# Attention probabilities transposed by a matmul with a diagonal matrix of row factors, in place of scaling on GpSimd and a transpose

## The reference

```
s = jnp.einsum('bhqd,bkhd->bhqk', qb, k) * scale      # plus bias / mask
p = softmax(where(valid, s, NEG))                     # exp(s - max) / sum
o = jnp.einsum('bhqk,bkhd->bqhd', p, v)               # o = g * (p @ v) in sel and win
```

## Time and profile before

| | us |
|---|---|
| median of 3 runs | 1456.19 |
| lowest and highest of them | 1454.94, 1457.26 |
| the profiled execution | 1460.9 |
| its span, first to last instruction | 1459.1 |
| attention of layer 0, first scores to last value product | about 101 to 160 |
| attention of layer 1, the same | about 830 to 875 |

### The profile page before, as it was taken

The page is one execution under the profiler, slowest core; times in us unless marked ns, Lnnn a source line. Parts: engine busy times, 40 slices in busy tenths (PEclk is TensorE's granted clock), DMA queues, the critical chain, the costliest instruction groups (busy, mean ns, idle before and its releaser), DMA issues.

```text
span 1459.1 us, 21577 instructions
## 1 busy us (share of the span) xinstructions
PE 1392.6 (95%) x8612; PEld 863.6 (59%) x8612; DVE 505.1 (35%) x834; ACT 356.4 (24%) x878; POOL 119.1 (8%) x155
## 2 busy tenths in 40 slices
PE   8977999999999999989999999999999999999878
PEld 3465576565656566654488466665656565666543
DVE  0387352333323323222610236232323323232253
ACT  1137132222222222212110242222222222222121
POOL 1229220000000000000100152100000000000000
PEclk9978999999999999999999989999999999999999
DMA  9540338999999999998563504599999999999951
GB/s 311 170 171 1 117 144 355 422 420 421 421 420 422 420 421 420 421 420 337 172 227 123 226 1 173 189 422 420 421 420 421 420 421 421 421 421 420 421 208 58
DMA packets 80806, 461.87 MB, mean 317 GB/s; under 512 B 9168, under 2 KB 9392, under 8 KB 30544
## 3 DMA queue, kind: packets, MB, share of 16 engines
q1 hardware_dynamic: 78128, 452.07, 76.3%
q0 software_dynamic: 2592, 8.53, 1.9%
HBM read 459.52 MB, written 1.05 MB: 316 GB/s over the span
## 4 chain that ended last, share of the span: by engine, by line
PE 90%; DVE 4%; POOL 2%; ACT 1%; issue 1%; DMA 0%; SPq 0%; DVEq 0%; ACTq 0%
PE ps L937 31%; PE ps L965 16%; PE ps L979 9%; PE ps L907 8%; PE ps L1083 4%; PE ps L644 4%; PE ps L688 3%; PE ps L803 3%; POOL roped L508 2%; PE ps L820 2%; PE ps L848 2%; PE ps L673 1%; PE ps L788 1%; PE ps L857 1%; PE ps L947 1%
## 5 line engine op out<-in xcount | busy, mean ns | idle before, releaser
L937 PE MATMUL ps<-ring,proj 128*64 128x256 f32 x2048 | 228.4, 381 | 5.9 <-issue 5.9
L965 PE MATMUL ps<-ring,qkT 128*64 128x512 f32 x1024 | 233.8, 598 | 0.0
L937 PEld LDWEIGHTS ps<-ring,proj 128*64 128x64 f32 x2048 | 152.2, 138 | 91.0 <-issue 25.4
L1693 DVE TENSOR_TENSOR o_tok<-ps,o_tok 128x1024 f32<-128x1024 f32 x128 | 156.6, 1224 | 103.8 <-PE ps L979 103.5
L1699 DVE TENSOR_TENSOR y_lo<-ps,y_hi 128x1024 fp32r<-128x1024 f32 x64 | 78.4, 1225 | 234.4 <-ACT y_hi L1283 234.4
L1685 DVE SCALAR_TENSOR_TENSOR roped<-roped,rows,ps 128x256 f32<-128x256 f32 x64 | 30.7, 480 | 318.1 <-ACT roped L1256 318.1
L965 PEld LDWEIGHTS ps<-ring,qkT 128*64 128x64 f32 x1024 | 67.8, 136 | 111.8 <-issue 110.4
L979 PE MATMUL ps<-y_hi,selT 128*128 128x512 f32 x256 | 113.2, 442 | 11.0 <-DVE o_tok L1693 7.5
L937 PE MATMUL ps<-ring,pT 128*64 128x256 f32 x1024 | 121.5, 379 | 2.2 <-ACT gb_row L1250 2.2
L1283 ACT ACTIVATE y_hi<-ps 128x1024 fp32r<-128x1024 f32 x64 | 65.5, 1024 | 234.5 <-PE ps L965 234.5
L937 PE MATMUL ps<-ring,gb_row 128*64 128x256 f32 x1024 | 121.5, 379 | 0.0
(11 more groups left out here) (247 smaller groups left out, 1497.2 us busy)
## 6 DMA issues: line engine op xcount, KB each, us to landing
ring<-in_exp_w_dram SPq DMA_DIRECT2D x384, 1024.0 KB, 13.4
ring<-in_od_w_in_dram SPq DMA_DIRECT2D x6, 2048.0 KB, 8.3
ring<-in_ple_w_gate_dram SPq DMA_DIRECT2D x4, 2048.0 KB, 11.1
ring<-in_ev_w_in_dram SPq DMA_DIRECT2D x3, 2048.0 KB, 21.5
ring<-in_sh_w_dram SPq DMA_DIRECT2D x6, 1024.0 KB, 7.0
ring<-in_ev_w_o_dram SPq DMA_DIRECT2D x2, 2048.0 KB, 10.7
ring<-in_od_w_o_dram SPq DMA_DIRECT2D x2, 2048.0 KB, 8.4
ring<-in_ev_w_in_dram SPq DMA_DIRECT2D x2, 1024.0 KB, 9.8
```

The lines of the kernel that those rows point to most:

```text
L937: ins = pe.matmul(ps[b * SLOTS:(b + 1) * SLOTS, 2, w * FE:(w + 1) * FE], xe(odd, c)[:, u * P + b * SLOTS:u * P + (b + 1) * SLOTS], views[b ...
L965: ins = pe.matmul(ps[b * SLOTS:(b + 1) * SLOTS, 4 + half, :], hT[:, f, b * SLOTS:(b + 1) * SLOTS], views[b][:, f, half * PIECE:(half + 1) ...
L1693: dve.tensor_tensor(y_acc[:, t, :], ps[:, bank:bank + 2, :].rearrange("p b n -> p (b n)"), y_acc[:, t, :], ALU.add)\
```

## The change

GpSimd no longer touches the scores. It builds, for each unit, four 128x128 diagonal matrices with the row factors on the diagonal, in one instruction: the identity, repeated four times, times `coef`, spread along the rows. Two such sets of four exist (`diag`, in `o_tok`, which is free in attention), so from the third unit on GpSimd also waits until TensorE has used the set of the unit before last. TensorE multiplies the block of unscaled probabilities (stationary) by the diagonal (moving), which gives the transposed and scaled block in the place where the transpose put it. The number of blocks, their PSUM places and the order of steps stay. DVE's guard on `coef` waits for the diagonal in place of the scaling.

```
-                for v, (what, t, g) in enumerate(UNITS[L % 2]):
-                    K = n_keys(t)
+                for v in range(len(UNITS[L % 2])):
                     pool.wait_ge(sem("sc_coef"), FIRST_UNIT[L] + v + 1)
-                    for s in range(4):
-                        part = scores[:, v % 4, s * K:(s + 1) * K]
-                        ins = pool.tensor_scalar(part, part, coef[:, v % 4, s:s + 1], None, ALU.mult)
-                    ins.then_inc(sem("sc_scaled"), 1)
+                    if v >= 2:
+
+                        pool.wait_ge(sem("unit_tp"), FIRST_UNIT[L] + v - 1)
+                    pool.tensor_tensor(diag[:, v % 2, :, :], ident.unsqueeze(1).to_broadcast([P, 4, P]),
+                                       coef[:, v % 4, :].unsqueeze(2).to_broadcast([P, 4, P]), ALU.mult)\
+                        .then_inc(sem("diag_built"), 1)
...
-                        pe.wait_ge(sem("sc_scaled"), B + v + 1)
+                        pe.wait_ge(sem("diag_built"), B + v + 1)
...
-                                ins = pe.transpose(ps[:, 4 + b // 4, (b % 4) * P:(b % 4 + 1) * P],
-                                                   scores[:, v % 4, s * n_keys(t) + c * P:s * n_keys(t) + (c + 1) * P],
-                                                   ident)
+                                ins = pe.matmul(ps[:, 4 + b // 4, (b % 4) * P:(b % 4 + 1) * P],
+                                                scores[:, v % 4, s * n_keys(t) + c * P:s * n_keys(t) + (c + 1) * P],
+                                                diag[:, v % 2, s, :], start=True, stop=True)
...
-                            dve.wait_ge(sem("sc_scaled"), B + v - 3)
+                            dve.wait_ge(sem("diag_built"), B + v - 3)
```

More of the change, by code:

```diff
@@ L173, in build_trunk @@
         y_acc = o_tok
+        diag = o_tok[:, 0, :].rearrange("p (u s n) -> p u s n", u=2, s=4)
         tmp_o = sb("tmp_o", 512)[:, :]
```

## The result

| | before | after |
|---|---|---|
| median, us | 1458.21 (15 runs) | 1461.62 (15 runs) |
| lowest and highest | 1454.94, 1462.52 | 1459.6, 1465.49 |
| the profiled execution | 1460.9 | 1460.05 |
| its span | 1459.1 | 1458.2 |
| layer 0, first scores to first product of the shared expert | 76.96 | 80.32 |

A forecast was written before the change was run, and what follows sets the result against it. TensorE was taken to make 90% of the chain, with GpSimd's scalings bounding part of layer 0's attention. Layer 0 +2.2 and layer 1 -1.4 gave +0.8 on 1456.19: 1457.0 us, range 1454.0 to 1460.7.

The forecast's parts named there:

- Start of layer 0, -1.1: Layer 0's first diagonal, taken at 1.27 us, is ready sooner than the scaled scores, so TensorE's first product starts 1.1 us earlier.
- Rival 2: Building the diagonal on GpSimd takes 2.87 us; layer 0 +2.9, layer 1 +2.0, total +4.9, 1461.1 us; chance 6%.
- The price of a product: On TensorE, products replacing transposes add 0.4 us per tile 0 unit, 0.87 per tile 1 unit, 0.7 at low clock.
- Idle time taken up, -4.7: In layer 0 the added TensorE work fills 4.7 of 5.9 us of its idle time, leaving 1.2.
- The tail, +1.75: From layer 0's output projection on, TensorE has no idle time, so units 10 and 11 add 1.75 us.
- Layer 0 together: Sum of layer 0's attention steps: +2.3 us, or +2.1 following each unit through all engines; taken as +2.2.
- Layer 1: Layer 1's attention: -2.4 us if the clock never falls, taken as -1.4 because timed runs may differ in clock falls.
- What lies outside, 0: After attention the chain is TensorE's to the end, so a shift passes through one to one, adding nothing.
- The base: The kernel before was taken at 1456.19 us, the median of three runs spread over 2.3 us.
- Rival 1: The clock brings no gain in layer 1; total +2.9 us, or +4.4 if earlier timed runs mostly had no fall; 14%.
- Rival 3: A product costs only a transpose's time on TensorE; layer 0 -2.6, layer 1 -7, 1446.6 us; chance 4%.
- Rival 4: Products keep the clock up where transposes do not; layer 0 +1.3, total about -1.1, 1455.1 us; chance 6%.

The follow-up runs named there:

- layer 0's half: The change in the 12 units of layer 0 alone, layer 1 as in the kernel before; ratios to before 1.0005, 1.0006 and 1.0004.
- products without diagonals: Kernel before, GpSimd still scaling, with only the transposes turned into products with the identity; ratio 1.0044, +6.4 us.
- filled kernel: Kernel before plus three unread 128x512 products in TensorE's idle time ahead of layer 1's first transpose; ratio 0.998 (-2.9 us), again 0.9984 (-2.3 us).

## Why the prediction was wrong

By its own steps:

- **Start of layer 0, -1.1.** The diagonal was taken at 1.27 and takes 1.04; the first product starts 9.31 us after the first scores, not 10.69. It was -1.4; 0.2 of the 0.3 beyond the forecast is the diagonal's. Rival 2, the dear diagonal, is dead.
- **The price of a product: the step that failed.** It said four or eight more records at 0.113 us "less a little overlap", and at low clock 0.7 us for four more. The rows of after have no such overlap, and the added records cost more: 0.12 to 0.13 us each at full clock, 0.24 at low clock. At full clock a unit of tile 0 goes to 1.09 and not 0.98, one of tile 1 to 1.86 to 1.99 and not 1.88 (+0.94 to +0.97 in place of +0.87), and at low clock the first two to 2.00 and not 1.75. In layer 0 up to the projection that is 2 x 0.25 - 0.2 (unit 2, of which part is already at full clock) + 3 x 0.11 + 4 x 0.08, or about +1.0. The first block of the projection starts 44.73 us after the first scores, before 43.19, so +1.5. The forecast's own items come to +0.55 there (it went on with 0.1 less). The rest of the difference is the start, 0.3 earlier, and 0.3 that was taken up less of idle time.
- **Idle time taken up, -4.7.** It held to 0.3. What is left is 0.48 before the second product and 0.33 and 0.19 before those of units 6 and 9, 1.0 in all and 1.3 with the drains, where the forecast left 1.2; and ACT's copy is what is late at all three.
- **The tail, +1.75.** The stage grows by 1.8 behind the first block. It held.
- Layer 0 together: +3.36 against +2.2. The same stage came at +3.2 to +3.5 in seven traces, those of the full change and of layer 0's half.
- **Layer 1.** -2.4 if the clock holds; it held, and the trace gives -1.7. Eight units were underpriced in the same way, by about 0.6 us together, which is most of the difference. The deduction to -1.4, for falls that timed runs might not have, came out near the trace by chance.
- **What lies outside, 0.** With the mis-sized price put right the forecast would be +3.4 - 1.7 = +1.7. Measured are +2.8, +2.5 and +1.8, whose intervals all hold 1.7, though two of the three lie about a us above it. If that us is real it belongs to the open part above. The -1.7 is against the one trace of before, with its two falls.
- **The base.** "1456.19 + 0.8" took the median of three runs with a spread of 2.3 us for the kernel's. It was 2.0 low, and the range was laid around it.

Rival 1 gave a time of 1459.1 to 1460.6 and a sign that came true, but not by its mechanism: the clock does bring its gain in the timed runs (filling the gap: -2.9, -2.3; mean clock 0.9809 to 0.9848). Rival 3 falls with sixteen records for eight blocks. Rival 4 asked whether products hold the clock up where transposes do not. The granted clock is back at 1.00 at 117.5 in after, 18.2 us after the first scores, and at 119.3 in before, 18.3 after them. Over all traces it is 17.8 to 18.5 us with diagonal products in the first units (seven traces) and 17.9 to 18.4 with transposes (seven); that shows no difference. The one trace of the products without diagonals stands apart: back at 113.9, 14.7 us after the first scores. It is a single execution, and whether the products did that is open. The Trainium skill, "TensorE: Matmul & The Clock Gate", section "Part 4: PE-mode transpose", says that full clock doesn't engage for the transpose mode, since it doesn't count as busy in the same way. In the filled kernel TensorE stays at full clock from the filling at 833.46 to 852.2, in steps a third of which are transposes, and falls behind an idle gap; so no run here shows a cost from that for mixed work. The Trainium skill, "Perfetto Trace Analysis", section "Transposes", which speaks for the transpose as its own instruction, was right here: an ordinary product costs 0.5 and 1.0 us more a unit.

## What to carry to other kernels

Give an engine that is being waited for relief only where it is waited for: the exchange of 2.5 us on GpSimd for 0.5 to 1.0 on TensorE lost 2.3 us applied to all units and won 3.9 applied to five (means of three and two measurements). Price an instruction that is doubled by doubling it (twice 0.59, 1.02 and 1.04 is within 0.1 of what was measured), and leave an overlap out unless a row shows it. And before a forecast of a few tenths of a per cent is laid on a median, look at how far its runs lie apart: three runs were 2 us off. A stage that repeats to 0.1 us in the traces where it is edited can still move by 3 us where it is not, so take several traces of the kernel before as well.

## What the runs showed of the hardware that I had not expected

- Three products whose result is not read, 2.8 us in an idle gap of TensorE, make the kernel 2.3 to 2.9 us faster. In both traces the stage's two falls of the clock become one, and another stands 14 us behind the stage, where it costs 1.56 us.
- The same gap of 2.55 us is followed by a fall of 6.8 us (before, layer 0's half again), or one of 3.4 that begins 0.8 or 2.4 us later (the other two traces of layer 0's half); behind a gap shortened to 1.2 us there is none, in seven traces. Three executions of one kernel, layer 0's half, give 60.34, 63.14 and 61.99 us for the same unedited stage.
- GpSimd's two-input product of 128x512 took 1.04 us with one operand constant along the row, 1.27 in the rotary step of the same size. What makes the difference was not isolated.
